# Reordering the vector, scalar and tensor queues around three normalisations in the last part of a two-block transformer kernel

## The reference, cut to what matters

```
# end of the first block
x = x + (silu(gp) * (h @ w_ffn_up)) @ w_ffn_down
# second block
h = rms_norm_2(x, mix_norm)                       # norm "sum2"
a, g = split(h @ a_w_in + a_b_in);  h = a * sigmoid(g)
h = causal depthwise conv of 31 taps(h) + conv_b
h = silu(layer_norm(h, ln_g, ln_b))               # norms "mu", "var"
x = x + h @ a_w_out + a_b_out
x = x + square(relu(rms_norm_2(x, mlp_norm) @ mlp_w1)) @ mlp_w2   # norm "sum3"
```

## Time and profile before

| | |
|---|---|
| median of 3 runs | 3369.89 us (3364.22 to 3376.41) |
| the profiled execution | 3384.76 us, its span 3382.9 us |
| busy share of the span | PE 94%, DVE 60%, ACT 32% |
| mean granted TensorE clock | 0.971 of full |
| panel high copy on ACT (line 284) | 1911 ns |
| panel low part on DVE (line 288) | 2295 ns |
| one tap on DVE (line 2583) | 749 ns |
| one add of `back_dve` (line 2760) | 686 ns |

### The profile page before, as it was taken

How to read it: one execution, slowest core, us unless ns; L and a number is a source line. 1 busy time by engine, 2 the same in 40 slices (tenths; PEclk the granted TensorE clock), 3 DMA queues, 4 the chain that set the end, 5 groups by cost and what they waited for, 6 DMA issues and landing times.

```text
span 3382.9 us, 52078 instructions
## 1 busy us (share of the span) xinstructions
PE 3193.5 (94%) x22004; PEld 2545.1 (75%) x22004; DVE 2035.6 (60%) x3235; ACT 1068.7 (32%) x1526; POOL 315.4 (9%) x307
## 2 busy tenths in 40 slices
PE   8999998788988888999999999999998999999999
PEld 7777786576766767778888888877746888778887
DVE  4665454577777775534544444448979987655445
ACT  5222334444444442221111111122153333433332
POOL 0222342000000000401000000000000000000000
PEclk9999999789999998999999999999999999999999
DMA  3342666234344433421111111111101222213222
GB/s 143 118 137 68 220 209 202 62 83 100 83 105 98 95 66 136 149 93 38 50 50 50 50 50 44 44 38 42 46 13 50 99 89 99 87 69 129 90 99 75
DMA packets 93527, 301.86 MB, mean 89 GB/s; under 512 B 10352, under 2 KB 38640, under 8 KB 70768
## 3 DMA queue, kind: packets, MB, share of 16 engines
q1 hardware_dynamic: 79104, 246.63, 23.5%
q0 software_dynamic: 14192, 51.91, 4.5%
HBM read 241.35 MB, written 57.15 MB: 88 GB/s over the span
## 4 chain that ended last, share of the span: by engine, by line
PE 78%; DVE 11%; issue 3%; ACT 3%; DMA 3%; POOL 2%; SPq 1%; DVEq 0%; ACTq 0%; POOLq 0%
PE ps L2414 24%; PE ps L308 20%; PE ps L503 6%; PE ps L1755 3%; PE ps L2239 2%; PE ps L2556 2%; PE ps L1766 1%; PE ps L2074 1%; PE ps L1778 1%; PE ps L475 1%; DVE Yh L2583 1%; PE ps L1423 1%; PE ps L1019 1%; DMA Dn<-nbs 1%; PE ps L2434 1%
## 5 line engine op out<-in xcount | busy, mean ns | idle before, releaser
L2414 PE MATMUL ps<-Hh,whi 128*128 128x512 f32 x1600 | 498.4, 393 | 0.0
L284 ACT ACTIVATE whi<-raw 128x2048 fp32r<-128x2048 f32 x139 | 265.7, 1911 | 638.3 <-PE ps L308 310.4
L288 DVE TENSOR_TENSOR wlo<-raw,whi 128x2048 fp32r<-128x2048 f32 x139 | 319.0, 2295 | 132.9 <-ACT whi L284 132.7
L2414 PEld LDWEIGHTS ps<-Hh,whi 128*128 128x128 f32 x1600 | 300.5, 188 | 68.0 <-issue 6.2
L2414 PE MATMUL ps<-Hh,wlo 128*128 128x512 f32 x800 | 311.6, 390 | 0.0
L2414 PE MATMUL ps<-aHh,whi 128*128 128x512 f32 x512 | 200.0, 391 | 3.6 <-DVE xT L2760 2.5
L308 PE MATMUL ps<-Hhi,wlo 128*128 128x512 f32 x656 | 202.2, 389 | 0.0
L308 PE MATMUL ps<-Hhi,whi 128*128 128x512 f32 x656 | 202.1, 389 | 0.0
L308 PE MATMUL ps<-Hlo,whi 128*128 128x512 f32 x656 | 202.1, 389 | 0.0
L2414 PE MATMUL ps<-aHh,wlo 128*128 128x512 f32 x512 | 199.4, 389 | 0.0
L2414 PE MATMUL ps<-aLh,whi 128*128 128x512 f32 x512 | 199.4, 389 | 0.0
(11 more groups left out here) (385 smaller groups left out, 6199.9 us busy)
## 6 DMA issues: line engine op xcount, KB each, us to landing
raw<-in_panels SPq DMA_DIRECT2D x139, 1024.0 KB, 4.7
rwf<-F POOLq DMA_DIRECT2D x16, 1280.0 KB, 6.8
L<-rwf SPq DMA_DIRECT2D x16, 1024.0 KB, 5.0
L<-rwf SPq DMA_DIRECT2D x64, 256.0 KB, 4.1
Dn<-nbs SPq DMA_DIRECT2D x128, 128.0 KB, 5.4
gts<-so POOLq DMA_DIRECT2D x16, 512.0 KB, 3.2
gl<-gts SPq DMA_DIRECT2D x32, 256.0 KB, 3.6
rwt<-so POOLq DMA_DIRECT2D x15, 512.0 KB, 3.0
```

Of the source, the lines that this page charges most:

```text
L284: e.activation(whi[i % 2][:, :], raw_of(i)[:, :], AF.Copy).then_inc(*a_hi.up(i))
L288: e.tensor_tensor(wlo[i % 2][:, :], raw_of(i)[:, :], whi[i % 2][:, :].bitcast(F32), OP.subtract).then_inc(*v_lo.up(i))
L2414: m = e.matmul(ap, W[wi][:, kc, n0:n0 + 128], mov[mi][:, kc, :], start=x == 0 and q == 0, stop=x == len(kcs) - 1 and q == 2)
```

## The change

Nothing is computed differently. Instructions change their place on DVE, ACT and PE.

At the join: `down_dve` of block 10 makes the first two low parts of the new stage before its add n = 6, and does not split a panel behind it. The split of ci1 (high copy on ACT, low part on DVE) stands behind chunk 4 of the first norm. PE waits for ci1 only ahead of its second group.

At half 0's first layer norm and sum3: `taps_act(1, 5)` goes ahead of the first silus. Behind outputs 6 and 7 of the projection DVE fills with 2 taps instead of 6, and with none between mean and reciprocal (there were 2); panel co3's split stands behind the mean on DVE and behind the last square on ACT; PE runs `taps_pe(1, 6)` before the last two sums.

At half 1's: four silus stay at b = 13, four go behind `up_act` of b = 14; the split of co0' goes ahead of the adds of b = 14; the last two sums go between the two outputs of `up_pe` of b = 15; mean, root and reciprocal follow the projection's last output on DVE and ACT, with the split of md14 between; chunks 0 to 3 are scaled inside b = 15, chunks 4 to 7 behind every second add of `back_dve(0, 15)`.

```diff
@@ down_dve, then ffn_act
     def down_dve(e, p, t, v, b):
         for n in range(8):
+            if b == 10 and n == 6:
+                first_lo_dve(e, 0, range(2))
             for h in range(2):
...
-        panels_after(panel_dve, e, p)
+        if b < 10:
+            panels_after(panel_dve, e, p)
...
-        panels_after(panel_act, e, UIX["fd10"])
@@ first_pe
         if h == 0:
             panel_pe(e, p)
-            panel_pe(e, p + 1)
...
+        if h == 0:
+            panel_pe(e, p + 1)
         for x, n0 in (("a", 0), ("gate", 128)):
@@ up_pe
                 half_pe(e, ("m", h, b, k), (a_e, "r", h, b, k), W, 128 * k, Gh[h], range(8))
+                if h == 0 and b == 15 and k == 0:
+                    last_pe(e, 1)
...
         co_pe(e, 0)                                       # late_pe
+        taps_pe(e, 1, 6)
         last_pe(e, 0)
-        taps_pe(e, 1, 6)
         taps_pe(e, 1, 7)
         for b in range(16):
             up_pe(e, 0, b)
-            if b == 15:
-                last_pe(e, 1)
@@ late_dve
-        first_lo_dve(e, 0, range(8))
+        first_lo_dve(e, 0, range(2, 5))
+        panels_after(panel_dve, e, UIX["fd10"])
+        first_lo_dve(e, 0, range(5, 8))
...
             co_dve(e, 0, n)
-            if n % 2:
+            if n in (1, 3, 5):
                 co_panel(panel_dve, e, 0, n // 2)
-            fill_dve(e, 6)
+            fill_dve(e, 6 if n < 6 else 2)
         mean_dve(e, ("sum3", 0), 0, 1e-6)
-        fill_dve(e, 2)
+        co_panel(panel_dve, e, 0, 3)
         recip_dve(e, ("sum3", 0), 0)
...
-            if b == 15:
-                mean_dve(e, ("sum3", 1), 1, 1e-6)
+            if b == 14:
+                panels_after(panel_dve, e, UIX["mu14"])
             for n in range(8):
                 if b:
                     back_dve(e, 0, b - 1, n)
+                if b == 14 and n < 4:
+                    silu_lo_dve(e, 1, n + 4)
                 fill_dve(e, 1)
-                if n == 1:
+                if n == 1 and b != 14:
                     panels_after(panel_dve, e, UIX[f"mu{b}"])
-                if b == 15 and n == 3:
-                    recip_dve(e, ("sum3", 1), 1)
+                if b == 15 and 2 <= n < 6:
+                    scaled_dve(e, 1, n - 2)
+                if b == 15 and 3 <= n < 7:
+                    scaled_lo_dve(e, 1, n - 3)
...
-                for ch in range(8):
+                for ch in range(4):
                     silu_lo_dve(e, 1, ch)
...
             if b == 14:
...
-                    if n % 2:
+                    if n in (1, 3, 5):
                         co_panel(panel_dve, e, 1, n // 2)
+                mean_dve(e, ("sum3", 1), 1, 1e-6)
+                co_panel(panel_dve, e, 1, 3)
+                recip_dve(e, ("sum3", 1), 1)
         panels_after(panel_dve, e, UIX["md14"])
-        scaled_dve(e, 1, 0)
         for n in range(8):
-            if n < 7:
-                scaled_dve(e, 1, n + 1)
-            scaled_lo_dve(e, 1, n)
+            if n % 2 == 0:
+                scaled_dve(e, 1, n // 2 + 4)
+                scaled_lo_dve(e, 1, n // 2 + 4)
             back_dve(e, 0, 15, n)
@@ late_act
-        first_act(e, 0)
+        first_act(e, 0, range(5))
+        panels_after(panel_act, e, UIX["fd10"])
+        first_act(e, 0, range(5, 8))
...
         root_act(e, ("var", 0), 0)
+        taps_act(e, 1, 5)
         silu_act(e, 0, range(2))
         y_act(e, 1, 3)
-        taps_act(e, 1, 5)
...
+            if b == 14:
+                silu_act(e, 1, range(4, 8))
+            if b == 15:
+                for kc in range(4):
+                    scaled_act(e, 1, kc)
...
             if b == 13:
                 root_act(e, ("var", 1), 1)
-                silu_act(e, 1)
+                silu_act(e, 1, range(4))
...
+                root_act(e, ("sum3", 1), 1)
+                co_panel(panel_act, e, 1, 3)
-        root_act(e, ("sum3", 1), 1)
-        for kc in range(8):
+        for kc in range(4, 8):
             scaled_act(e, 1, kc)
```

More of the change, by code:

```diff
@@ L2434, in sums_pe, with first_act @@
             e.matmul(ring.bank(*key), ones, src(kc), start=kc == 0, stop=kc == 7).then_inc(*t_e.up(*key, kc))
-    def first_act(e, h):
-        for kc in range(8):
+    def first_act(e, h, kcs=range(8)):
+        for kc in kcs:
             e.wait_ge(*v_ff.by("x", 10, kc, h))
@@ L2929, in late_act @@
         for n in range(0, 8, 2):
-            co_panel(panel_act, e, 0, n // 2)
+            if n < 6:
+                co_panel(panel_act, e, 0, n // 2)
             last_act(e, 0, n)
             last_act(e, 0, n + 1)
+        co_panel(panel_act, e, 0, 3)
         root_act(e, ("sum3", 0), 0)
@@ L2945, in late_act @@
                 root_act(e, ("var", 1), 1)
-                silu_act(e, 1)
+                silu_act(e, 1, range(4))
             if b == 14:
                 for n in range(0, 8, 2):
-                    co_panel(panel_act, e, 1, n // 2)
+                    if n < 6:
+                        co_panel(panel_act, e, 1, n // 2)
                     last_act(e, 1, n)
                     last_act(e, 1, n + 1)
-        root_act(e, ("sum3", 1), 1)
-        for kc in range(8):
+                root_act(e, ("sum3", 1), 1)
+                co_panel(panel_act, e, 1, 3)
+        for kc in range(4, 8):
             scaled_act(e, 1, kc)
```

## The result

| | before | after |
|---|---|---|
| median of 4 runs, us | 3368.01 | 3346.49 |
| ratio of times to before | | 0.9925 (95%: 0.9907 to 0.9943) |
| span of the profiled execution, us | 3382.9 | 3345.6 |
| mean granted clock | 0.971 | 0.977 |

The ratio is 25 us of 3368; 25.4 were forecast, and a median of 3344.5. The medians as shown lie 21.5 us apart, the two profiled spans 37.3. Four marks on TensorE sort this out: A is the start of the last matmul of fd10, B the first matmul of the second group of the first stage, C the first matmul of half 0's MLP, D the first matmul of the second panel of half 1's MLP. The table gives the distances in us, read from the start times in each trace.

A forecast was written before the change was run, and what follows sets the result against it. PE, busy 94% of the span, was taken as the bound, with 28.3 us of waits in the changed part. Join 7.3, half 0 8.2 and half 1 9.9 sum to 25.4 us, from 3369.89 to 3344.5; range 3335 to 3357.

The forecast's parts named there:

- Join, 7.3 us: At the join: PE starts 4.6 us earlier, and 2.7 us more come from having no half-clock stretch.
- the moved split: At the join: low part 5, behind ci1's split, just fits PE's need; a miss costs up to 0.5 us.
- Half 0, 8.2 us: At half 0's norms: reciprocal 8.0 us earlier, so PE starts the MLP at 2597.2 instead of 2605.45.
- PE's pauses: At half 0's sum3: about 1.5 us before square 6, 1.2 before square 7, 4.4 before the MLP.
- The share that the prediction gave to them, 0.76 us: At half 0's layer norm: with diagonals moved ahead, DVE gains only its short waits for silus, 0.76 us.
- Half 1, 9.9 us: At half 1's norms: mu1' is split by 3032.2 instead of 3042.05, 9.9 us earlier, including 2.33 from co0'.
- The wait for co0': At half 1's projection: with four silus moved, co0' is split sooner and PE starts 2.33 us earlier.
- md14's wait: In half 1, at down block 14: PE waits about 0.8 us for md14's low part.
- New waits in half 1: Rival at half 1: late banks or mu0' leave only co0''s 2.3 us; 17.8 us in all, 3352; chance 0.12.
- the clock stays down: Rival at half 0's norm: pauses keep half clock through chunk 7's taps; gain 21.4 us, time 3348.5; chance 0.2.
- The MLP loop took the 10 taps: In half 0's MLP loop: moved taps stay hidden, DVE about 19 us per b against 21.8 us of matmuls.
- Nothing was slower: Rival at half 1: md14 ready after 3022.5 loses the whole gain; 3380 us and up; chance 0.02.

The follow-up runs named there:

- pe_wait_only: Kernel before with only PE's wait for panel ci1 moved behind the first group; 3368.16 us, one run.
- order0_only: Kernel before with only half 0's orders changed (diagonals, chunk 6's taps, panel split), all taps staying where they were on DVE; 3365.83 us, one run.
- after_again: The changed kernel run and profiled a second time, with an empty diff; 3344.04 us, 0.9926 of the kernel before.
- silus_only: Kernel before with only four silus moved behind the relus of b = 14 and co0' split ahead of its adds; 3372.08 us, one run.
- sums_first: fewer_taps with the two last sums on PE put back ahead of the taps of chunk 6; 3343.95 us, 0.9913 of the kernel before.
- y_behind: sums_first with ACT's y of chunk 7 moved behind the eight copies of scaled chunks; 3343.06 us, 0.9924 of the kernel before.
- fewer_taps: Changed kernel with 8 more taps of half 1 moved from ahead of half 0's sum3 into the MLP loop; 3346.41 us, 0.9924 of the kernel before.
- recip_first: Changed kernel with the reciprocal of half 1's sum3 ahead of panel md14's split on DVE; 3361.66 us, one run.
- join_only: Kernel before with only the join's edits; 3368.17 us, 0.9992 of the kernel before.

## Why the prediction was right, point by point

**Join, 7.3 us: measured 7.26.** The pause and the half-clock stretch both went. The tight spot was the moved split: DVE left ci1's low part at 2236.88, low part 5 followed, and PE took chunk 5 with no wait in its list. pe_wait_only shows that PE's part of the edit alone gains 0.3 to 0.8 us; that each other part was needed too is argued from the timelines and not shown.

**Half 0, 8.2 us: measured 8.26.** PE's pauses are 1.3 and 1.0 us at the squares and 4.2 ahead of the MLP (1.5, 1.2 and 4.4 forecast). The reciprocal starts 7.55 us behind output 6's add, the MLP 5.67 us behind the reciprocal's start (5.65 by the prediction's times). The diagonals cost nothing in their new place. The share that the prediction gave to them, 0.76 us, can only be set beside order0_only's 1.1, where the other orders changed too. The table load and root followed each other 1.29 us apart, from 2570.38 to 2571.67, with no drain. By the Trainium skill, "ScalarE: Activation LUTs", section "What ACT_TABLE_LOAD costs", a load has one of about 1.38 us, and this trace does not agree with it. The split ended at 2572.6 and the root at 2572.3, so 0.3 us of it would have been hidden here and 1.1 us would have shown.

**Half 1, 9.9 us: measured 10.16 in the first profile, 9.1 in after_again.** The wait for co0' went (2.3 us forecast, 2.4 in silus_only), md14's wait is 0.2 us (0.8 forecast), mu1''s 0.6 (under 1 forecast), the two waits for banks went but for 0.2 us, and mu1' sets D: its split ends at 3004.72, D is 3004.77. The panel whose copy at 3012.84 held the old root is mu0', not md15 as the prediction has it: ACT's copies stand in the order of the panels, and md15's is the one ahead. No number hangs on the name. Between the two profiles the difference is 1.05 us and is the length of the half-clock stretch at C, 3.4 or 6.8 us; it belongs to C and not to half 1. That the first profile has the same 3.4 us there as the kernel before is luck; with the second the three places come to 24.6 us instead of 25.7.

**The rivals.** New waits in half 1 did not come. That the clock stays down came in part: not in the taps, but at the MLP's start, where 4.2 us of pause were left. Its price can be read: half 1's MLP starts 413.9 us behind C with no such stretch (sums_first, y_behind), 414.75 with 3.4 us of it and 415.8 to 416.3 with 6.8. Only the step from 414.75 to 415.80 is between traces of one kernel. The MLP loop took the 10 taps with no change that these stretches do not explain, and 8 more with 0.5 us at most (fewer_taps against after_again). Nothing was slower.

**Where my expectations failed.** In fewer_taps I moved the bound off DVE and did not ask what would be late next on PE; the same in sums_first for ACT. Both are the same omission: the queue of the engine that had been waiting. In recip_first I gave a wait of the list to the wrong panel, since two panels share its line.

## What to carry to other kernels

A wait that the profile names on the busy engine is often the last link; follow it to the order of the queues of the other engines, and move all the links together: PE's alone gave 0.3 to 0.8 of 7.3 us here. Where a list of waits goes by line, look up in the timeline which panel a wait is for. After each wait removed, walk every in-order queue once more for the instruction that now stands ahead of the critical one. Where code far ahead of the change scatters by more than the change is worth, compare traces between marks around the change and not spans: here A to B repeats within 0.02 us in the traces where it runs at full clock and within 0.5 us where it does not, while A itself scatters by 20 us.

## What the runs showed of the hardware that was not expected

The stretch at half clock behind the same pause of 4.2 us lasted 3.4 us in one profile of the changed kernel and 6.8 us in the next, with all matmul starts from A to it the same to 0.04 us; here is the second one (its window answers to 2577.80:2581.10 of the first):

```profile
2586.90:2593.50 6.60, 5.03 (x12) 3.99 (x13) 6.15 (x11) 3.15 (x5) 0.00 (x0) 0.50 0.01 4
2593.50:2600.00 6.50, 6.50 (x30) 5.39 (x29) 6.12 (x10) 1.90 (x3) 0.00 (x0) 0.99 0.01 3
```

It costs 1.05 us more. In the kernel before, a pause of 3.5 us, a sum and a pause of 3.2 us brought 10.2 us at half; in join_only the same code had pauses of 1.0 and 4.1 us there and 6.8 us at half. The changed kernel's pauses of 1.3 and 1.0 us at the same place brought none.
